# Attention maps divided by their sums on GpSimd ahead of the transposes, instead of spreading the sums with TensorE

## What is computed

```python
s = jnp.where(mask, q @ k.T * scale, NEG)
p = jax.nn.softmax(s, axis=-1)          # exp(s - max) / sum
o = p @ v
# the window attention has one more logit per head, the sink, in max and sum alone
```

## Time and profile before

| | |
|---|---|
| Median of 3 runs | 2762.84 us (2756.43 to 2764.87) |
| Profiled execution | 2761.17 us |
| Its span | 2759.4 us, mean granted TensorE clock 0.985 |
| TensorE matmul queue | 2658.5 us busy, 96% |
| VectorE | 1555.9 us, 56% |
| ScalarE | 1139.5 us, 41% |
| GpSimd | 129.8 us, 5% |
| DMA | 205 MB, mean 74 GB/s |

### The profile page before, as it was taken

One profiled execution on the slowest core, in us unless ns is written; L12 is line 12 of the kernel. 1 busy time (PEld: TensorE's weight loads), 2 busy tenths in 40 slices (PEclk: granted clock), 3 DMA queues, 4 the chain that ended last, 5 costly groups with the idle time before them and its releaser, 6 DMA issues. The chain is left out here.

```text
span 2759.4 us, 40735 instructions
## 1 busy us (share of the span) xinstructions
PE 2658.5 (96%) x15744; PEld 2217.8 (80%) x15744; DVE 1555.9 (56%) x3335; ACT 1139.5 (41%) x2522; POOL 129.8 (5%) x140
## 2 busy tenths in 40 slices
PE   7999999999999999999999999999998899999998
PEld 7889989899988877878876677888786657788887
DVE  5365656655545555655678463443567875533446
ACT  3345332543333443343435553332355564432333
POOL 1001000000100100000013000000003300000000
PEclk9999999999999999999999999999999899999999
DMA  3201212123220221223321122323231102222333
GB/s 132 82 29 54 66 39 81 58 74 92 85 77 28 67 58 57 82 62 93 97 84 56 43 84 82 100 93 98 92 93 44 48 1 77 86 98 96 95 96 96
DMA packets 115265, 205.33 MB, mean 74 GB/s; under 512 B 13824, under 2 KB 23680, under 8 KB 114944
## 3 DMA queue, kind: packets, MB, share of 16 engines
q1 hardware_dynamic: 114064, 200.14, 23.8%
q10 hardware_dynamic: 1008, 2.59, 0.3%
HBM read 200.51 MB, written 2.10 MB: 73 GB/s over the span
## 5 line engine op out<-in xcount | busy, mean ns | idle before, releaser
L2348 PE MATMUL pp<-Hh,wh 128*128 128x512 f32 (+1 forms) x2336 | 857.9, 367 | 36.0 <-DVE Hl L1892 15.8
L2349 PE MATMUL pp<-Hl,wh 128*128 128x512 f32 (+1 forms) x2336 | 803.4, 344 | 0.0
L2350 PE MATMUL pp<-Hh,wl 128*128 128x512 f32 (+1 forms) x2336 | 803.2, 344 | 0.0
L1861 DVE TENSOR_TENSOR wl<-raw,wh 128x512 fp32r<-128x512 f32 (+2 forms) x738 | 481.9, 678 | 412.9 <-ACT wh L1660 402.1
L1660 ACT ACTIVATE wh<-raw 128x512 fp32r<-128x512 f32 (+2 forms) x774 | 451.3, 605 | 349.1 <-PE pp L2350 286.6
L2348 PEld LDWEIGHTS pp<-Hh,wh 128*128 128x128 f32 x2336 | 444.9, 190 | 119.1 <-DVE Hl L1892 18.1
L2350 PEld LDWEIGHTS pp<-Hh,wl 128*128 128x128 f32 x2336 | 444.4, 190 | 52.0
L2349 PEld LDWEIGHTS pp<-Hl,wh 128*128 128x128 f32 x2336 | 446.0, 191 | 49.8
L2348 PE MATMUL pp<-Yh,wh 128*128 128x512 f32 (+1 forms) x1222 | 452.9, 371 | 3.0 <-DVE wl L1861 1.8
L2349 PE MATMUL pp<-Yl,wh 128*128 128x512 f32 (+1 forms) x1222 | 436.1, 357 | 0.0
L2350 PE MATMUL pp<-Yh,wl 128*128 128x512 f32 (+1 forms) x1222 | 436.0, 357 | 0.0
(11 more groups left out here) (279 smaller groups left out, 2818.1 us busy)
## 6 DMA issues: line engine op xcount, KB each, us to landing
raw<-in_w SPq DMA_DIRECT2D x698, 256.0 KB, 2.6
raw<-in_w SPq DMA_DIRECT2D x36, 192.0 KB, 2.4
raw<-in_w SPq DMA_DIRECT2D x40, 128.0 KB, 2.1
out<-X SPq DMA_DIRECT2D x8, 256.0 KB, 2.0
con<-in_con SPq DMA_DIRECT2D x1, 1513.0 KB, 7.1
X<-in_x SPq DMA_DIRECT2D x2, 528.0 KB, 5.6
X<-in_x ACTq DMA_DIRECT2D x2, 528.0 KB, 6.6
Z<-in_p ACTq DMA_DIRECT2D x2, 512.0 KB, 3.3
```

The lines of the kernel that those rows point to most:

```text
L1861: e.tensor_tensor(part("wl", j), landing(j), part("wh", j).bitcast(F), ALU.subtract).then_inc(*dve.up("split", j))
L2348: e.matmul(it.ps, wh, xh, start=it.first, stop=False)
L2349: e.matmul(it.ps, wh, xl, start=False, stop=False)
L2350: e.matmul(it.ps, wl, xh, start=False, stop=it.end).then_inc(*pe.up())
```

## The change

The maps are divided before they are transposed. In round n, right behind the scores of unit n, the new kind `divide` is issued for unit n-1: VectorE inverts that unit's one sum (with a sink it first adds the one column), and GpSimd multiplies the map in SBUF, 128 queries by up to 528 keys, by that column. The transposes of that unit, a round later, wait for GpSimd instead of for ScalarE's exponential. After the last unit of a list the divide comes in the first round without scores. Differential units keep their mix.

`inverse`, `spread`, `spread out`, `spread z` and `times out` go. In the first network one VectorE pass, `gated out`, multiplies the output in bank 6 by the gate. In the second `high` and `low` read the output from its bank, which is free after `low`; it was free after `times out`.

```diff
-            if halves and "end" in u:
-                u["inverse"] = do("inverse", sums=u["all"], exp=u["exp"], alle=u["alle"] if "sink" in u else None, sink=n)["n"]
+
+        def divide(u):
+            n = u["n"]
+            do("divide", u=n, p=u["p"][0], sum=u["sums"][0], exp=u["exp"], sink=u["sink"][1] if "sink" in u else None)
+            u["exp"] = ("pool", "divided", n)
...
-            if halves and "end" in u:
-                u["spread"] = do("spread", sums=u["all"], ident=ident, ps=bank(5), free=free[5], inverse=u["inverse"])["n"]
...
                 if pend1 and "mix" in u:
                     pend1[-1]["exp"] = u["mix"](pend1[-1])
+                elif pend1:
+                    divide(pend1[-1])
                 pend1.append(u)
...
+            elif len(pend1) == deep:
+                if "mix" in heads[-1]:
+                    heads[-1]["exp"] = heads[-1]["mix"](heads[-1])
+                else:
+                    divide(heads[-1])
...
-                f = do("spread z", ...)
-                free[5] = ("dve", "evac", f)
-                yield
-                f = do("times out", ...)
+                f = do("gated out", q=q, ps=bank(6)[...], z=Z[:, :, a:a + qr], t=t, turned=tmp_turned["at"])["n"]
...
# finish2
-            o = m["O"][:, :]
-            f = do("spread out", dst=o, ps=bank(5), spread=u["spread"], turned=turned["o"])["n"]
-            free[5] = ("act", "evac", f)
+            fields = high_part(bank(bk).rearrange("p (c n) -> p c n", c=4), yh[:, :, a:a + 128], yl[:, :, a:a + 128], t)
             yield
-            f = do("times out", q=o, ps=bank(bk), t=t, by=free[5])["n"]
-            free[bk] = ("dve", "evac", f)
-            yield
...
+            free[bk] = low_part(fields)
...
# VectorE
+    def divide(it):
         dve.wait_ge(*it.exp)
+        if it.sink is not None:
+            dve.wait_ge("act", "sink", it.u)
+            e.tensor_tensor(it.sum, it.sum, it.sink, ALU.add).then_inc(*dve.up())
             dve.wait_ge("dve")
+        e.reciprocal(it.sum, it.sum).then_inc(*dve.up("inverse", it.u))
+
+    def gated_out(it):
+        dve.wait_ge("dve")
+        dve.wait_ge(*it.t)
         if it.turned:
             dve.wait_ge(*it.turned)
         e.tensor_tensor(it.q, it.ps, it.z, ALU.mult).then_inc(*dve.up("evac", it.n))
...
# GpSimd
+    def divide(it):
+        pool.wait_ge("pool")
+        pool.wait_ge("dve", "inverse", it.u)
+        e.tensor_scalar(it.p, it.p, it.sum, None, ALU.mult).then_inc(*pool.up("divided", it.u))
...
# TensorE
-    def spread(it):
-        pe.wait_ge("dve", "inverse", it.inverse)
-        if it.free:
-            pe.wait_ge(*it.free)
-        for h in range(8):
-            c, half = divmod(h, 2)
-            done = e.matmul(it.ps[64 * half:64 * half + 64, 128 * c:128 * c + 128], it.sums[:, h:h + 1].to_broadcast([128, 64]), it.ident, start=True, stop=True)
-        done.then_inc(*pe.up("spread", it.n))
```

More of the change, by code:

```diff
@@ L2267, in vector_program @@
             "rows there": rows_there, "relu2": relu2, "relu2 low": relu2_low, "add_out": add_out, "add_normed": add_normed, "final": final, "ple": ple, "scores": scores,
-            "turn": turn, "inverse": inverse, "spread z": spread_z, "times out": times_out, "negs": negs, "lambda": lam, "mix": mix, "diff out": diff_out,
+            "turn": turn, "divide": divide, "gated out": gated_out, "negs": negs, "lambda": lam, "mix": mix, "diff out": diff_out,
             "diff norm": diff_norm, "diff scale": diff_scale, "index_key": index_key, "index_w": index_w, "query squares": query_squares, "weighed sums": weighed_sums, "query factors": query_factors, "query scales": query_scales, "index": index,
@@ L2314, in rope_halves @@
             e.tensor_tensor(it.dst, it.dst, it.p, ALU.add).then_inc(*pool.up("rope halves", it.key))
+    def divide(it):
+        pool.wait_ge("pool")
+        pool.wait_ge("dve", "inverse", it.u)
+        e.tensor_scalar(it.p, it.p, it.sum, None, ALU.mult).then_inc(*pool.up("divided", it.u))
     def mark(it):
         pool.note("mark", it.n)
-    does = {"mark": mark, "ones rows": ones_rows, "key ropes": key_ropes, "rope halves": rope_halves, "split": split, "heads out": heads_out}
+    does = {"mark": mark, "ones rows": ones_rows, "key ropes": key_ropes, "rope halves": rope_halves, "split": split, "heads out": heads_out, "divide": divide}
     return schedule(m, m["PP"], does)
@@ L2490, in tensor_program @@
     does = {"mark": mark, "load": load, "panel": panel, "step": step, "norm_total": norm_total, "norm_col": norm_col, "norm sums": norm_col, "query squares": norm_col, "weighed sums": weighed_sums, "norm_rows": norm_rows, "rows there": rows_there, "scores": scores,
-            "turn": turn, "product": product, "products": products, "spread": spread, "turn_out": turn_out, "turn_v": turn_v, "index_w": index_w, "index": index}
+            "turn": turn, "product": product, "products": products, "turn_out": turn_out, "turn_v": turn_v, "index_w": index_w, "index": index}
     return schedule(m, m["PP"], does)
```

31 lines of the change are left out of this document (3 added, 28 removed).

## The result

The changed kernel takes 2783.71 us in the median of 4 runs (2780.41 to 2787.32), the kernel before on the same chip 2762.22. The ratio is 1.0082, with an interval of 1.0067 to 1.0097: slower by 0.7 to 1.0%, 21.5 us. The prediction was 2758, in a range of 2739 to 2782. It is wrong in sign and size, and the measured median lies 1.7 us outside the range. The profiled execution took 2786.73 us around a span of 2784.5.

A forecast was written before the change was run, and what follows sets the result against it. TensorE, busy 96% of the span, was taken as the bound; gains of 42 us against costs of 11, 10, 9, 3 and 4 gave -5 us, a median of 2758 us, in a range of 2739 to 2782.

The forecast's parts named there:

- the price of the divide: GpSimd's multiply of a map: about 0.7 us at 512 columns, between 0.6 and 1.3.
- The ring: Last mixer from 2236 on, engines waiting in turn: 13 gaps too short, 9 us lost (7.5 to 14.6).
- The last mixer until 2236: Reciprocals late behind top-k and score passes, partly absorbed by TensorE's own waits: 10 us lost, bounds 4 and 16.
- GpSimd's queue: Until 2205 of the last mixer, divides stand behind weight splits and key copies: 3 us, bounds 0 and 8.
- Another half-clock stretch: In the last mixer, clock already 0.87: a sign that the forecast is wrong, given no size.
- Outside the last mixer: 22 of 248 gaps too short, most at a stage's first maps: 11 us lost (8.7 to 17.4).
- the two engines holding each other up: VectorE's two-input work does not run beside GpSimd: 19 us of VectorE, 4 us taken as cost, bounds 0 and 12.
- The gains: Spreads gone 35.9 us, waits in front 3, banks free sooner 3: 42 us together (36 to 46.5).
- Rival 2: Slower: the divide costs as much as a two-input operation, in last mixer and stages' first maps; 2781 us, chance 0.20.
- The long gap: In the last mixer from 2236 on, once per two maps: 1.5 us, fits the new way's need of about 1.05.
- Rival 3: Slower: each of 19 us of VectorE delay reaches TensorE through late weight splits or score passes; 2773 us, chance 0.07.
- The rule that spoke against the change: Skill page: elementwise work belongs on VectorE, GpSimd about twice as slow with two inputs; by it the sum is +13 us.

The follow-up runs named there:

- undivided: The changed kernel without any division: no reciprocals, sink additions or GpSimd multiplies, transposes waiting for the exponentials as before; 2715.17 us, ratio 0.9837 to the kernel before.
- early: The changed kernel with, in the last mixer alone, each map's reciprocal and divide queued right behind its exponential; 2766.77 us, ratio 1.002 to the kernel before.
- broadcast: The changed kernel with GpSimd's multiply as a two-operand operation, the sum spread over the columns; 2758.65 us, ratio 0.9993 to the kernel before.

## Why the prediction was wrong

**The step that failed** is the price of the divide: "I take it near the copy, since it has one tensor input". The number of tensor inputs doesn't tell this operation's price. It is the slowest elementwise row of GpSimd here, above both neighbours that bounded it: at 512 columns 1.58 us, against 0.61 for the copy and 1.33 for the subtraction of the earlier trace rows. The two nearest rows were no bounds, because both were of other kinds of instruction. The need at 512 columns became 1.86 us instead of 1.05.

**The ring** was right as a mechanism, wrong by that price. I had 9 us (7.5 to 14.6). It takes 57.8 us before (2236.21 to 2293.98), 54.6 in `undivided` and 74.2 after: a cost of 19.6. Had 0.36 been held against 1.86, each short gap would have lacked 1.5, and 13 of them, the shorter maps less, some 16 to 19. The rows to predict this were there, except for the one duration. TensorE's waits for GpSimd are 16.0 of the 19.6.

**The last mixer until 2236** had 10 us, and 3 for GpSimd's queue. It costs 15.4 (80.4 in `undivided`, 95.8 after); what GpSimd's queue has of it was not told apart. Here also the mechanism was named and is seen: the first divide starts 2.6 us after its exponential, since the reciprocal stands behind top-k passes and the next score pass.

```profile
2148.86 0.19 ACT L1773 ACTIVATION_READ_ACCUMULATOR P<-P,st 128x1 f32 x1
...
2151.27 0.16 DVE L2121 RECIPROCAL st<-st 128x1 f32<-128x1 f32 x1
...
2151.60 0.60 POOL L2301 TENSOR_SCALAR P<-P,st 128x128 f32<-128x128 f32 x1 [2.41 <-DVE st L2121]
...
2152.26 0.48 PE L2402 MATMUL pp<-con,P 128*128 128x128 f32 x1 [6.14 <-POOL P L2301]
```

In the earlier trace rows TensorE waited 2.98 and then 2.23 us at this point, 5.2 together; now it waits 6.14 at once. So the delay of the first map was nearly absorbed, as I had put it. The hand-overs were 0.17 us into GpSimd and 0.06 into TensorE, together what I had allowed. What was not in the sum is the clock. "Another half-clock stretch" stood in the prediction as a thing that would make it wrong, but without a price: it came, with 24 us more at half clock than before and 20.5 more than in `undivided`, and is a third of this stage's cost. Most of it lies ahead of the ring, 42.9 us against 27.3 in `undivided`, and there it is about half of the 15.4.

**Outside the last mixer** I had 11 us (8.7 to 17.4) and 4 for the two engines holding each other up. It came to 35.6 in these executions: 9.2 in the dilated attention and 26.4 in the first network. TensorE's own waits for GpSimd are 13.3 us in the first network and 11.0 in the dilated attention, so the short gaps were there, and cost more by the price. The dilated attention is a second ring like the last mixer's, where TensorE had 2.0 us idle in 61.4 before and has 11.1 in 68.2 now; I hadn't looked at it by itself. And the first network too has its slow stretches now. For its first attention, after and then `undivided`:

```profile
129.00:219.00 90.00, 82.94 (x641) 69.22 (x640) 53.44 (x211) 36.97 (x113) 41.16 (x40) 0.96 0.09 26
```

```profile
128.00:210.00 82.00, 79.65 (x648) 67.53 (x647) 50.31 (x173) 37.36 (x113) 0.00 (x0) 1.00 0.10 28
```

Of the 8 us, 4.7 are idle time and 3.3 are slower matmuls. Over the six attentions TensorE's idle time is 12.2 us more than in `undivided`, and 20.7 us more are at half clock, which is about 10 us of slower work; some 4 us are left unexplained. Since the same instructions had only 15.2 us at half clock in `early`, a part of this, 4 us there, belongs to the execution and not to the change.

**The gains** were 47 us instead of 42, just over their upper bound: the waits around the spreads were worth more than the 6 of 10.6 that I took.

**The range** stopped at 2782 though the bounds of the terms, -26.5 and +32, reach 2795 from the median before. I had written that the range takes them in but for their last few microseconds; at the upper end it leaves out 13, and the measured time lies there.

**Rival 2** came nearest: "the divide costs as much as a two-input operation", with 2781 and a chance of 0.20. Its mechanism is what the runs show (the divide costs even more, 1.58 us against 1.33), but that its number fits is partly luck, since its gains were 5 us too low and its costs of 60 were 8.5 too low, with no clock among them. Its threshold, "a 512-column divide of about 1.0 us on", was low: the two-operand form stands at 1.06 us and comes out level with the kernel before. The long gap held up even at 1.58.

**Rival 3**, the two engines holding each other up, happens, but through late weight splits it costs TensorE nothing that shows. VectorE's weight splits of 512 columns take 0.693 us when no divide runs. The first two pairs of lines are from after, a divide that starts during a split and a split that starts during a divide; the third is from `broadcast`, the same with the two-operand form:

```profile
388.38 0.67 DVE L1850 TENSOR_TENSOR wl<-raw,wh 128x512 fp32r<-128x512 f32 x1
388.63 1.90 POOL L2301 TENSOR_SCALAR P<-P,st 128x528 f32<-128x528 f32 x1 [4.26 <-DVE st L2121]
...
404.81 1.61 POOL L2301 TENSOR_SCALAR P<-P,st 128x528 f32<-128x528 f32 x1 [4.11 <-DVE st L2121]
405.23 0.83 DVE L1850 TENSOR_TENSOR wl<-raw,wh 128x512 fp32r<-128x512 f32 x1
```

```profile
1053.44 1.07 POOL L2301 TENSOR_TENSOR P<-P,st 128x528 f32<-128x528 f32 x1 [0.69 <-DVE st L2121]
1053.79 1.26 DVE L1850 TENSOR_TENSOR wl<-raw,wh 128x512 fp32r<-128x512 f32 x1
```

Where the split starts first (20 divides in each of the two kernels), GpSimd pays: its divide takes longer, mostly by 0.29 to 0.30 us (1.90 instead of 1.61 above, with 0.42 left of the split). Where the divide starts first, the form decides. Beside the two-operand form 15 of 17 splits ended 0.55 us after the divide's end and took 0.93 us in the mean, at most 1.26. Beside the one-tensor form the 29 such splits took 0.71 in the mean and at most 0.90, and 7 of them ended while the divide still ran. The Trainium skill, "SBUF — State Buffer" (SBUF: two separate sides), says that the shared port pair is an exclusive lock, held for the whole instruction by whichever engine starts first. The traces agree where the split is first, and with the two-operand form both ways; for a divide of the one-tensor form that is first they don't, and there the measurement decides. The 1.46 us of the earlier trace rows stood beside a two-operand product too. TensorE's waits for these splits don't change: 11.0 us in 14 places after and in `undivided`, 10.9 in 14 in `broadcast`, 9.5 in 13 before. What the 20 late divides cost it was not tried.

**The rule that spoke against the change** held in its effect: the multiply of 512 columns takes 0.49 us on VectorE and 1.58 on GpSimd. The Trainium skill, "GPSIMD Engine Reference" (Engine selection), says that GpSimd is about half as fast with two inputs and "1-input is roughly line-rate". By it the one-tensor form should have been the fast one. The trace has it the other way round: 1.58 us with one tensor input, 1.06 with two.

## What to carry to other kernels

The cost of an instruction that no row shows is bounded by the same kind of instruction, not by one with as many operands; where there is none, the range has to reach well past the neighbours, and the forms that compute the same should be timed against each other first, which was worth 25 us here (for the faster form the row was there, 1.10 us). In a ring of engines, a new step costs its whole way (queue, hand-overs, duration) less the gap that is there, once per turn: the gap is read from the timeline, every stage that has such a ring gets its own term, and where the step stands in each queue can matter as much as how long it takes (17 us in one stage). The half clock deserves a term in the sum and not only a warning: in the last mixer it was a third of the cost, and the same instructions had more or less of it from one execution to the next.

## What the runs showed of the hardware

- On GpSimd a multiply of an fp32 map of 128 partitions by a column takes 0.62, 0.97 and 1.58 us at 128, 256 and 512 columns in its one-tensor form, 0.42, 0.64 and 1.06 as two operands with the column spread by its pattern. With a constant instead of the column it is 1.51 at 512.
- On VectorE the same one-tensor form takes 0.49 us at 512 columns, 0.38 at 256.
- From VectorE's reciprocal to GpSimd's start passed 0.16 us, and 0.06 from GpSimd's end to TensorE's.
- A GpSimd divide that starts during a weight split on VectorE takes mostly 0.29 us longer. A split that starts during a divide waits for its end if the divide has two operands (0.93 us in the mean instead of 0.69), and not if it has one tensor (0.71).
- In the six attentions of the first network the same instructions, with TensorE idle 25 us each time, took 585.9 us with 25.7 us at 1.2 GHz and 581.6 with 15.2.
- In the last mixer TensorE spent 24 us more at 1.2 GHz after than before, and was idle 21 us more (13.7 to 34.5).
